# A top-k attention on one core: the next head's third logits ahead of the transposes of the third query tile

## The reference

```python
score = jnp.einsum('bqhs,bqh->bqs', jax.nn.relu(s_idx), wb)
score = jnp.where(admissible[None], score, -jnp.inf)
top_val, top_idx = lax.top_k(score, n_sel)                   # n_sel = 128
q_lat = jnp.einsum('bqhd,hcd->bqhc', qb, w_uk)
logits = jnp.einsum('bqhc,bqkc->bhqk', q_lat, c_sel) * ATT_HEAD_DIM ** -0.5
logits = logits + jnp.moveaxis(rel_bias[rel_bucket(top_idx - qpos[None, :, None])], -1, 1)
p = jax.nn.softmax(logits, axis=-1)
u = jnp.einsum('bhqk,bqkc->bqhc', p, c_sel)
o = jnp.einsum('bqhc,hcd->bqhd', u, w_uv)                    # then o @ w_out
```

## Time and profile before

| what | value |
|---|---|
| median of 3 runs | 2103.38 us |
| lowest and highest of the 3 | 2101.78 and 2106.79 us |
| the profiled execution's own time | 2099.49 us |
| its span | 2097.7 us |
| TensorE busy | 2013.8 us (96%) |
| VectorE busy | 1051.5 us (50%) |
| ScalarE busy | 745.5 us (36%) |
| mean granted clock of TensorE | 0.978 of full speed |

### The profile page before, as it was taken

One profiled execution on the slowest core, in us unless ns is written; L12 is line 12 of the kernel. 1 busy time (PEld: TensorE's weight loads), 2 busy tenths in 40 slices (PEclk: granted clock), 3 DMA queues, 4 the chain that ended last, 5 costly groups with the idle time before them and its releaser, 6 DMA issues.

```text
span 2097.7 us, 28613 instructions
## 1 busy us (share of the span) xinstructions
PE 2013.8 (96%) x11546; PEld 1725.7 (82%) x11546; DVE 1051.5 (50%) x1348; ACT 745.5 (36%) x941; POOL 248.5 (12%) x208
## 2 busy tenths in 40 slices
PE   8999988999999999999999999999997899999996
PEld 6788765788888878998999999998884588888885
DVE  6668665544444544131543434345897553444434
ACT  4449734423132443223332222223535442222122
POOL 2012230200000210013100000001245010000001
PEclk9999999999999998998999999999998999999998
DMA  4223211222222221111222222222121022222221
GB/s 173 101 81 114 71 49 41 100 90 92 101 99 82 101 81 52 69 41 41 81 81 100 81 100 81 98 83 101 61 91 51 21 86 95 101 96 84 101 100 60
DMA packets 27823, 174.67 MB, mean 83 GB/s; under 512 B 4409, under 2 KB 4537, under 8 KB 7762
## 3 DMA queue, kind: packets, MB, share of 16 engines
q1 hardware_dynamic: 25680, 167.32, 22.5%
q0 software_dynamic: 1888, 5.90, 0.9%
q10 hardware_dynamic: 162, 0.10, 0.0%
HBM read 171.19 MB, written 4.78 MB: 84 GB/s over the span
## 4 chain that ended last, share of the span: by engine, by line
PE 70%; issue 20%; DVE 5%; ACT 3%; POOL 2%; DMA 1%; SPq 0%; POOLq 0%; DVEq 0%; ACTq 0%
PE lin L448 57%; PE aux L1302 1%; PE aux L2176 1%; POOL squares L629 1%; ACT w_hi L363 1%; PE aux L1745 1%; PE aux L1759 1%; PE lin L1257 1%; PE lin L2146 1%; PE aux L2160 1%; DMA w_raw<-in_weights 1%; PE aux L1286 1%; DVE w_lo L370 1%; PE aux L1773 0%; PE aux L2024 0%
## 5 line engine op out<-in xcount | busy, mean ns | idle before, releaser
L448 PE MATMUL lin<-v_hi,w_hi 128*128 128x264 f32 (+1 forms) x1712 | 573.9, 335 | 4.8 <-DVE v_lo L614 3.5
L448 PE MATMUL lin<-v_hi,w_lo 128*128 128x264 f32 (+1 forms) x1712 | 571.1, 334 | 0.0
L448 PE MATMUL lin<-v_lo,w_hi 128*128 128x264 f32 (+1 forms) x1712 | 569.5, 333 | 0.0
L448 PE MATMUL lin<-x_hi,w_hi 128*128 128x512 f32 (+1 forms) x1176 | 417.0, 355 | 15.8 <-DVE tmp L542 6.6
L370 DVE TENSOR_TENSOR w_lo<-w_raw,w_hi 128x2048 fp32r<-128x2048 f32 (+1 forms) x144 | 328.5, 2281 | 187.0 <-ACT w_hi L363 186.8
L448 PE MATMUL lin<-x_hi,w_lo 128*128 128x512 f32 (+1 forms) x1176 | 413.7, 352 | 0.0
L448 PE MATMUL lin<-x_lo,w_hi 128*128 128x512 f32 (+1 forms) x1176 | 413.4, 352 | 0.0
L363 ACT ACTIVATE w_hi<-w_raw 128x2048 fp32r<-128x2048 f32 (+1 forms) x155 | 292.9, 1890 | 281.4 <-PE lin L448 274.3
L448 PEld LDWEIGHTS lin<-v_hi,w_hi 128*128 128x128 f32 x1712 | 324.6, 190 | 40.4 <-DVE v_lo L614 4.3
L448 PEld LDWEIGHTS lin<-v_lo,w_hi 128*128 128x128 f32 x1712 | 324.3, 189 | 33.6 <-issue 0.7
L448 PEld LDWEIGHTS lin<-v_hi,w_lo 128*128 128x128 f32 x1712 | 324.3, 189 | 32.1
(11 more groups left out here) (375 smaller groups left out, 2351.7 us busy)
## 6 DMA issues: line engine op xcount, KB each, us to landing
w_raw<-in_weights SPq DMA_DIRECT2D x155, 1024.0 KB, 4.8
rel_by_distance<-rel_by_distance POOLq DMA_DIRECT2D x1, 2599.5 KB, 20.9
rel_bias<-rel_by_distance POOLq DMA_DIRECT2D x8, 264.0 KB, 3.0
h<-in_x_t SPq DMA_DIRECT2D x4, 512.0 KB, 8.1
out_t<-h SPq DMA_DIRECT2D x4, 512.0 KB, 2.8
o_t<-in_mem_t POOLq DMA_DIRECT2D x1, 1024.0 KB, 5.0
cst<-in_consts SPq DMA_DIRECT2D x1, 512.0 KB, 9.8
col<-in_cols ACTq DMA_DIRECT2D x1, 67.0 KB, 5.8
```

Source lines behind the costliest of these rows:

```text
L448: last = nc.tensor.matmul(o, a, b, start=(k % (L.kc // k_banks) == 0 and p == 0), stop=((k + 1) % (L.kc // k_banks) == 0 and p == 2))
```

## The change

Two lines of `pe_attend` change places with one: in every head but the last, L3 is written ahead of T3. Its semaphore wait moves with it. The number of instructions and all other engines' queues stay as they are.

```diff
                 turned(hd, 2)
                 if hd:
                     mix(hd - 1, (0, 1))
-                turned(hd, 3)
                 if more:
                     logits(hd + 1, (3,))
+                turned(hd, 3)
                 if hd:
                     mix(hd - 1, (2, 3, 4))
                 turned(hd, 4)
```

## The result

The changed kernel takes 2104.95 us in the median of 20 runs (2102.65 to 2106.93), and the kernel before 2101.18 us in the median of 20 (2094.29 to 2107.07). The ratio is 1.0017, with a 95% interval of 1.0009 to 1.0025: some 3.6 us slower, and the interval leaves no room for the small gain that was forecast. The profiled execution took 2106.93 us, with a span of 2105.1 us.

The account below looks back on a forecast made before the run. TensorE was taken to bound the kernel behind the attention, and a TensorE-VectorE ring of 8.85 us each undisturbed head. Head 0's -0.4 us plus zeros elsewhere, put on the median, gave 2103.0 us, range 2098.8 to 2107.0 us.

Parts of the forecast that it names:

- Head 0: L3 fills TensorE's 0.63 us idle before T3; T3 0.53 us later, T4 0.61 earlier; gain 0.3 to 0.6 us, taken as 0.4.
- ring of head 0: Head 0's loop from T2 to the next T2: 0.30 us of the 0.61 us reach biased 4 if the clock's return stays.
- Heads 1 to 6: T3 and L3 take 1.12 us in either order on TensorE, so the change is 0, within -0.6 to +0.6 us.
- undisturbed head: A head at full clock takes 8.85 us, 6.46 on TensorE plus 2.39 mainly on VectorE, and stays so.
- biased 3 was released by the transposes: On VectorE, biased 3 still starts at 1619.77, released by T3 in place of the logits; the wait is not shortened.
- ScalarE's cover: On ScalarE, 0.31 us remain between exp 2's new end at 1620.76 and the copy to `x_hi` at 1621.07.
- bound of 0.1 us for the new neighbours: TensorE seams M01 then L3, L3 then T3, T3 then M234 change at most 0.1 us a head either way; taken as 0.
- -0.4 (head 0) + 0 (six heads) + 0 (head 7, untouched): Whole kernel: 0.4 us won, 2099.1 us for the profiled execution's like, 2103.0 us when put on the median.
- untouched: Head 7 is not altered by the change, so its term in the forecast is 0 us.
- own last sign of being wrong: In the profile after, a different number of heads with a mean clock under 1 would show the prediction wrong.
- Rival 6: Clock falls more often in heads 1 to 6, work bunched, head 0's end shifted; three more low stretches, 2108.1 us; chance 0.07.
- Rival 2: Clock returns earlier in head 0 without the 0.63 us pause: 1.6 to 3.3 us won, 2100.1 to 2101.8 us; chance 0.10.

Follow-up runs that it names:

- first pair of profiles: First profiled executions of the kernel before (2099.49 us) and the changed kernel (2106.93 us); medians 2101.18 and 2104.95 us.
- second pair: Both original kernels run and profiled once more, nothing altered: changed 2104.18 us (ratio 1.0008), before 2101.58 us (0.9999).
- fuller filling: Repeated or unread logits added in TensorE's pauses in heads 0 to 7: on the changed kernel 2094.23 us (0.9965), on the kernel before 2093.83 us (0.9964).
- four profiles at 13.3 to 13.45 us: By clock's fall to T2 of head 1: changed with two transposes more 2104.10 us, before 2101.18 and again 2101.58, exchange in heads 1 to 6 2101.40.
- all ten profiles of the table: Profiles with unfilled pauses: both kernels twice, each half of the exchange, two or six repeated transposes, T4 cut in head 0; medians 2096.66 to 2104.95 us.

## Why the prediction was wrong

**Head 0: right.** T3 came 0.50 us later (0.53 worked out), L4 0.64 us earlier (0.61), and the ring of head 0 0.27 us shorter in the first pair of profiles and 0.34 in the second (0.30 was worked out where the clock returns at an unmoved instant).

**Heads 1 to 6: right as far as the order goes.** The undisturbed head stayed at 8.85 us, biased 3 was released by the transposes, and ScalarE's cover was 0.31 us. The exchange in these heads alone changed nothing (0.9999, 0.9990 to 1.0008). The bound of 0.1 us for the new neighbours was not needed.

**The step that failed** is the sum, "-0.4 (head 0) + 0 (six heads) + 0 (head 7, untouched)", put on the median as if the clock's losses behind head 0 were scatter about the same middle. They are not scatter: the two zeros hold for the order of the instructions, but not for the clock. What shortened head 0 by 0.3 us also moved heads 1 to 7 against the clock's changes, which stayed where they were (10.24 and 23.9 us behind the fall ahead of head 0, in both kernels), and here the new place is a worse one: T2 of head 0 to the next layer takes 80.4 to 80.6 us against 74.0 to 77.4 us, most of it in the tail behind T2 of head 7. Head 7 was called untouched, and it holds 3.3 us of the loss. The prediction's own last sign of being wrong was there too: the mean clock is under 1 in five heads after (0, 2, 3, 5 and 7), and in four and three in the two profiles of the kernel before.

**Rival 6** named the place ("head 0's end shifts against the instants at which the clock changes"), but put it beside the bunching of the new order, asked for three more low stretches and gave it 0.07. The shift was right and the bunching wrong. In the first pair of profiles the one stretched head more is given back by head 5, and the tail alone turns the sign. In the second pair heads 3 and 5 cost 1.7 us each and the tail 3.4 us, together 6.4 us with head 0's gain taken off. The range of 2098.8 to 2107.0 us held the time, because the clock's scatter had been put into it. That, and a difference under the 0.2% to which it gave 0.86, say nothing for its mechanism.

**Rival 2,** that taking out a pause helps the clock, is refuted for head 0's pause: from T2 to T2 the mean clock of head 0 is 0.67 to 0.68 after and 0.69 before, and the clock returned 10.24 us behind its fall with and without the pause. But the fuller filling took all low stretches out of the attention in the profile of the changed kernel, and all but one in that of the kernel before. With that agrees what is said of another kernel in the Trainium skill, "TensorE: Matmul & The Clock Gate", section "A second HAM failure mode: psum-queue depth-cycling", that small pauses between groups of matmuls make the clock swing.

**What stays open.** The four profiles at 13.3 to 13.45 us show three different sets of stretches (74.0, 76.9 and 77.3 to 77.4 us), so near an edge the outcome differs between executions of one kernel. The two profiles of the kernel before, at 13.38 and 13.41 us, are an example. Whether the order of heads 1 to 6 has a share in that is not settled. How often each kernel lands on which side is not shown either, because only one execution of each comparison was profiled. Nor do the runs show why the clock falls in one turn of the loop and not in the next.

## What to carry to other kernels

Where TensorE's clock swings between its levels, a small gain ahead of such a part of the program need not arrive at the end. It also moves the work behind it against the clock's changes, and that was worth up to 8 us here for 0.3 to 0.7 us of shift, in either direction. Judge such an edit by the undisturbed repetitions of the loop, and ask for the time only after the pauses are filled, here by repeating matmuls whose result is the same. Before believing in a mechanism for a difference of a few microseconds, run the kernel with a delay of a few tenths of a microsecond and nothing else.

## What was not expected of the hardware

The clock fell at the same place of the program every time: 4.9 to 5.1 us ahead of T2 of head 0 in all ten profiles of the table, though T2 itself came at 1588.1 to 1592.5 us. That fits with a shift of 0.3 us inside head 0 giving the same stretches in two profiles of the changed kernel and in two other kernels (80.43 to 80.55 us), in place of drowning in scatter. And more work for TensorE made the kernel faster: six transposes in one head 7.5 us, and the fuller filling, with 32 more matmul records in the attention than the changed kernel (305 against 273), brought a median some 10 us below the changed kernel's.
